# The first modulation set of a transformer block loaded in two halves, with three weight units between them

## The reference

```python
c_act = jax.nn.silu(c)
mod = c_act @ w_ada[l] + b_ada[l]
sh1, sc1, g1, sh2, sc2, g2, sh3, sc3, g3 = jnp.split(mod, N_MOD, axis=-1)
hn = _modulate(_rms(h, norm_ffn1[l]), sh1, sc1)
h = h + 0.5 * g1[:, None, :] * _swiglu(hn, ffn1_w1[l], ffn1_w3[l], ffn1_w2[l])
```

## Time and profile before

| | us |
|---|---|
| median of 3 runs | 2513.48 |
| lowest, highest | 2511.37, 2516.77 |
| the profiled execution's own time | 2513.98 |
| its span | 2512.2 |
| TensorE busy | 2482.2 |
| VectorE busy | 1857.6 |
| ScalarE busy | 1167.3 |
| GpSimd busy | 127.9 |

### The profile page before, as it was taken

How to read it: one execution, slowest core, us unless ns; L and a number is a source line. 1 busy time by engine, 2 the same in 40 slices (tenths; PEclk the granted TensorE clock), 3 DMA queues, 4 the chain that set the end, 5 groups by cost and what they waited for, 6 DMA issues and landing times.

```text
span 2512.2 us, 33153 instructions
## 1 busy us (share of the span) xinstructions
PE 2482.2 (99%) x12155; PEld 2092.3 (83%) x12155; DVE 1857.6 (74%) x2078; ACT 1167.3 (46%) x1423; POOL 127.9 (5%) x198
## 2 busy tenths in 40 slices
PE   7999999999999999999999999999999999999999
PEld 5888888888889999897888888888787888888887
DVE  6876679898978988887865676777689655555556
ACT  4544444444447555655555444344543444444443
POOL 4210000000000000000000000000000000000000
PEclk9999999999999999999999999999999999999999
DMA  9986679999986878875544788786598776676775
GB/s 372 385 277 189 189 256 366 315 361 312 365 284 212 286 257 276 266 224 153 160 141 142 250 263 279 256 297 230 175 350 295 226 209 209 209 209 209 210 211 173
DMA packets 286595, 631.23 MB, mean 251 GB/s; under 512 B 24866, under 2 KB 25476, under 8 KB 285572
## 3 DMA queue, kind: packets, MB, share of 16 engines
q1 hardware_dynamic: 269600, 571.41, 69.2%
q0 software_dynamic: 15120, 53.51, 6.3%
q10 hardware_dynamic: 1748, 4.62, 0.5%
HBM read 616.82 MB, written 12.64 MB: 251 GB/s over the span
## 4 chain that ended last, share of the span: by engine, by line
PE 90%; DVE 5%; DMA 3%; issue 1%; ACT 1%; ACTq 0%; POOL 0%; DVEq 0%
PE psum L2337 26%; PE psum L2339 25%; PE psum L2338 25%; PE psum L2637 3%; PE psum L2639 3%; PE psum L2638 3%; PE psum L2675 2%; DVE w_lo L1472 1%; PE psum L2325 1%; DMA raw<-in_ffn_w 1%; DMA aT_raw<-act_bands 1%; DVE ada_acc L1492 0%; DMA act_bands<-act_blk 0%; DMA gate_mix<-gate_rows 0%; DVE ada_acc L1586 0%
## 5 line engine op out<-in xcount | busy, mean ns | idle before, releaser
L1472 DVE TENSOR_TENSOR w_lo<-raw,w_hi 128x1024 fp32r<-128x1024 f32 (+1 forms) x850 | 1033.6, 1220 | 498.1 <-ACT w_hi L948 496.8
L948 ACT ACTIVATE w_hi<-raw 128x1024 fp32r<-128x1024 f32 (+1 forms) x850 | 898.6, 1060 | 1024.8 <-PE psum L2339 831.2
L2337 PE MATMUL psum<-w_hi,xT_hi 128*128 128x512 f32 x1984 | 783.3, 395 | 3.4 <-issue 2.9
L2339 PE MATMUL psum<-w_hi,xT_lo 128*128 128x512 f32 x1984 | 773.7, 390 | 0.0
L2338 PE MATMUL psum<-w_lo,xT_hi 128*128 128x512 f32 x1984 | 773.5, 390 | 0.0
L2337 PEld LDWEIGHTS psum<-w_hi,xT_hi 128*128 128x128 f32 x1984 | 373.1, 188 | 86.9 <-issue 9.2
L2339 PEld LDWEIGHTS psum<-w_hi,xT_lo 128*128 128x128 f32 x1984 | 373.0, 188 | 78.6
L2338 PEld LDWEIGHTS psum<-w_lo,xT_hi 128*128 128x128 f32 x1984 | 373.1, 188 | 76.3
L2337 PE MATMUL psum<-w_hi,aT_hi 128*128 128x512 f32 x704 | 276.2, 392 | 4.2 <-DVE aT_lo L1745 3.5
L2338 PE MATMUL psum<-w_lo,aT_hi 128*128 128x512 f32 x704 | 275.1, 391 | 0.0
L2339 PE MATMUL psum<-w_hi,aT_lo 128*128 128x512 f32 x704 | 275.0, 391 | 0.0
(11 more groups left out here) (278 smaller groups left out, 2031.9 us busy)
## 6 DMA issues: line engine op xcount, KB each, us to landing
raw<-in_ffn_w SPq DMA_DIRECT2D x528, 512.0 KB, 4.5
ada_raw<-in_w_ada SPq DMA_DIRECT2D x224, 512.0 KB, 5.9
raw<-in_w_in SPq DMA_DIRECT2D x224, 512.0 KB, 3.9
ada_raw<-in_w_ada POOLq DMA_DIRECT2D x32, 512.0 KB, 7.0
ada_more<-in_w_ada POOLq DMA_DIRECT2D x32, 512.0 KB, 7.4
raw<-in_w_br_ssd SPq DMA_DIRECT2D x32, 512.0 KB, 5.5
raw<-in_w_br_att SPq DMA_DIRECT2D x32, 512.0 KB, 4.6
raw<-in_w_out SPq DMA_DIRECT2D x32, 512.0 KB, 5.3
```

The source lines that it names most:

```text
L948: nc.scalar.activation(w_hi[:, n.slot(SPLIT), 0:size], raw[:, n.slot(RAW), 0:size], ACT.Copy).then_inc(hi_ready, 1)
L1472: nc.vector.tensor_tensor(w_lo[:, n.slot(SPLIT), 0:size], raw[:, n.slot(RAW), 0:size], w_hi[:, n.slot(SPLIT), 0:size], ALU.subtract).then_ ...
L2337: nc.tensor.matmul(o, hi[:, kt + k, toks], whi, start=a, stop=False)
L2339: ins = nc.tensor.matmul(o, lo[:, kt + k, toks], whi, start=False, stop=b)
```

## The change

1. Set 0 (tiles 0 to 3) becomes two sets of two tiles (one pair each), of 8 pieces each. A piece still holds 512 KB, now of two tiles of rows by 512 columns, and is loaded with two DMAs of 256 KB and used with two VectorE instructions. There are five sets; the sums go to banks 4, 6, 4, 5, 4. Piece 7 is no longer TensorE's.
2. TensorE transposes two pairs, sums the first half, transposes two more, and does units 0, 1 and 2 (w1 block 0, w3 block 0, w3 block 1, all of pair 0); the other four pairs are transposed in front of units 1, 2 and 3; three warm-ups, the sum of the second half and two warm-ups stand in front of unit 3. The transposes go to banks 6, 7.
3. VectorE's list has the splits of units 0 to 3 behind pieces 7, 9, 11 and 13, ahead of mod_first there. SyncE loads the first units when the pieces before 3, 6, 8 and 11 are used. GpSimd computes the root behind 8 pieces. ScalarE's copies of x are spread between the casts.
4. Another order of units: both first pairs of eight blocks come ahead of the sum for tiles 4 to 7 (now in front of unit 15), then w1 block 4 with four, and w3 block 2, w1 block 3 and w3 block 3 with two more units each. These three are added to their part sums on VectorE. The later sums stand in front of units 30 and 44.

```diff
-ADA_SHARE = (1, 4, 7)
+ADA_SHARE = (1, 4)
...
-    SET_TILES = ((0, 4), (4, 4), (8, 4), (12, 4))
-    SET_START = (0, 16, 32, 48, 64)
+    SET_TILES = ((0, 2), (2, 2), (4, 4), (8, 4), (12, 4))
+    SET_START = (0, 8, 16, 32, 48, 64)
+    SUM_BANK = (4, 6, 4, 5, 4)
...
-    EARLY = (some("w3", 1, (0, 1)) + some("w1", 0, (0,)) + some("w1", 2, (0, 1)) + some("w1", 0, (1,))
-             + some("w3", 2, (0, 1)) + some("w3", 0, (0,)) + some("w1", 3, (0, 1)) + some("w3", 0, (1,))
-             + some("w1", 1, (0, 1))
-             + some("w3", 3, range(4)) + some("w1", 0, (2,)) + some("w1", 4, range(4)) + some("w1", 0, (3,))
-             + some("w3", 0, (2, 3)) + some("w1", 1, (2, 3))
+    EARLY = (some("w1", 0, (0,)) + some("w3", 0, (0,)) + some("w3", 1, (0, 1)) + some("w1", 0, (1,))
+             + some("w1", 2, (0, 1)) + some("w3", 0, (1,)) + some("w3", 2, (0, 1)) + some("w1", 1, (0,))
+             + some("w1", 3, (0, 1)) + some("w3", 3, (0, 1)) + some("w1", 1, (1,))
+             + some("w1", 4, range(4)) + some("w1", 0, (2,)) + some("w3", 2, (2, 3)) + some("w3", 0, (2,))
+             + some("w1", 3, (2, 3)) + some("w1", 0, (3,)) + some("w3", 3, (2, 3)) + some("w3", 0, (3,))
+             + some("w1", 1, (2, 3))
...
-             + some("w3", 2, range(2, UPB)) + some("w1", 3, range(2, UPB)) + some("w2", 2, range(UPB))
-             + some("w3", 3, range(4, UPB)) + some("w1", 4, range(4, UPB)) + some("w2", 3, range(UPB))
+             + some("w3", 2, range(4, UPB)) + some("w1", 3, range(4, UPB)) + some("w3", 3, range(4, UPB))
+             + some("w2", 2, range(UPB)) + some("w1", 4, range(4, UPB)) + some("w2", 3, range(UPB))
...
-    ADDED = [(0, at_unit["w3", 1, 5], 4), (1, at_unit["w1", 2, 5], 4), (0, at_unit["w3", 1, 7], 4),
+    ADDED = [(2, at_unit["w3", 2, 3], 4), (3, at_unit["w1", 3, 3], 4), (4, at_unit["w3", 3, 3], 4),
+             (0, at_unit["w3", 1, 5], 4), (1, at_unit["w1", 2, 5], 4), (0, at_unit["w3", 1, 7], 4),
...
-    SUM_AT = {at_unit["w1", 1, 0]: 1, at_unit["w1", 1, 2]: 2, at_unit["w1", 1, 4]: 3}
+    SUM_AT = {at_unit["w1", 1, 1]: 2, at_unit["w1", 1, 2]: 3, at_unit["w1", 1, 4]: 4}
...
-    SPLIT_AFTER = (14, 16, 17, 18, 20, 21, 22, 23, 25, 26, 27, 28, 31, 32, 33, 34, 35, 36, 37, 38, 39, 41, 42, 43, 44,
-                   46, 47, 48, 49, 50, 51, 52, 53, 54, 55, 57, 58, 59, 60, 62, 63)
-    SCALE_AFTER = (15, 32, 48)
-    ROWS_AFTER = (16, 17, 33, 34, 49, 50)
-    FIRST_UNITS_AFTER = (10, 12, 14, 15)
+    SPLIT_AFTER = (7, 9, 11, 13, 17, 18, 19, 20, 21, 22, 23, 25, 26, 27, 28, 29, 30,
+                   32, 33, 34, 35, 36, 37, 38, 39, 40, 41, 42, 43, 44, 45, 46, 47,
+                   48, 49, 50, 51, 52, 53, 54, 55, 56, 58, 59, 60, 62, 63)
+    SCALE_AFTER = (7, 15, 32, 48)
+    ROWS_AFTER = (8, 17, 33, 34, 49, 50)
+    FIRST_UNITS_AFTER = (3, 6, 8, 11)
...
-        for m in range(ADA_DEEP + 2):
+        for m in range(ADA_DEEP):
             load_first(m)
         pool.wait_ge(sums_ready, 1)
         inverse_root(rstd[:], rbase[:], row_sums[:], D, rstd_ready)
...
-            for j in range(UPB):
+            for j in range(2):
                 stage(0, j)
-            cast_units(2)
+            cast_units(1)
             rows_of_set(0)
-            cast_units(SPLIT)
+            for u in range(1, SPLIT):
+                cast_units(u + 1)
+                for j in (2 * u, 2 * u + 1):
+                    stage(0, j)
+            rows_of_set(1)
...
-                if m == 8:
+                if m == 6:
                     columns()
+                if m in SPLIT_AFTER and m < SET_START[2]:
+                    early_step(SPLIT_AFTER.index(m))
                 if m in SCALE_AFTER:
                     mod_first(SCALE_AFTER.index(m))
                 if m in ROWS_AFTER:
                     lo(0, ROWS_AFTER.index(m))
-                if m in SPLIT_AFTER:
+                if m in SPLIT_AFTER and m >= SET_START[2]:
                     early_step(SPLIT_AFTER.index(m))
...
         share(ADA_SHARE[1])
-        share(ADA_SHARE[2])
         warm_up(1)
         pe.wait_ge(xn_ready, 2)
-        for j in range(UPB):
-            if j >= 2:
-                pe.wait_ge(staged, j - 1)
-            turn_x(0, j, y)
-        for m in (9, 11, 13, 15):
-            pe.wait_ge(ada_used, ada_own(m))
-            warm_up(1)
+        for j in range(2):
+            turn_normed(j)
         sum_first(0)
-        warm_up(2)
+        for j in (2, 3):
+            turn_normed(j)
...
                 if n in SUM_AT:
                     e = SUM_AT[n]
-                    if e < SETS - 1:
-                        pe.wait_ge(part_kept, (4, 6)[e - 1])
+                    if e == 2:
+                        pe.wait_ge(part_kept, 5)
                     else:
-                        pe.wait_ge(part_added, 2)
+                        pe.wait_ge(part_added, 3 if e == 3 else 5)
                     sum_first(e)
+                if n == 1:
+                    turn_normed(4)
+                if n == 2:
+                    turn_normed(5)
+                if n == 3:
+                    turn_normed(6)
+                    turn_normed(7)
+                    pe.wait_ge(staged, UPB)
+                    for m in (11, 13, 15):
+                        pe.wait_ge(ada_used, ada_own(m))
+                        warm_up(1)
+                    sum_first(1)
+                    warm_up(2)
...
+                    if n == at_unit["w3", 2, 2]:
+                        pe.wait_ge(part_kept, 6)
+                    if n == at_unit["w1", 3, 2]:
+                        pe.wait_ge(part_added, 1)
+                    if n == at_unit["w3", 3, 2]:
+                        pe.wait_ge(part_added, 2)
```

More of the change, by code:

```diff
@@ L629, in first_sources_of, with pairs_of_set @@
         return [row[:, :, tile * P:(tile + count) * P] for row in rows]
+    def pairs_of_set(e):
+        tile, count = SET_TILES[e]
+        return range(tile // 2, (tile + count) // 2)
     def landed_first(m):
@@ L679, in turn_bank @@
     def turn_bank(f, j):
-        return (0 if f == 2 else 2) + j % 2
+        return (6, 2, 0)[f] + j % 2
     def twice(cols):
@@ L886, in _ @@
         inverse_root(rstd[:], rbase[:], row_sums[:], D, rstd_ready)
-        for m in range(ADA_DEEP + 2, PIECES):
+        for m in range(ADA_DEEP, PIECES):
             load_first(m)
@@ L1027, in rows_of_set @@
             act.wait_ge(scale_ready, e + 1)
-            for j in (2 * e, 2 * e + 1):
+            for j in pairs_of_set(e):
                 if j >= 2:
@@ L1044, in silu_kept @@
         def silu_kept(o, i):
-            act.wait_ge(part_added, [a[0] for a in ADDED[2:]].index(i) + 3)
+            act.wait_ge(part_added, [a[0] for a in ADDED[PART_SUMS:]].index(i) + PART_SUMS + 1)
             act.wait_ge(prod_ready, o)
@@ L1530, in mod_first @@
             dve.wait_ge(ada_summed, e + 1)
-            nc.vector.tensor_tensor(both(modT), psum[:, 4 + e % 2, 0:2 * count].rearrange("p (c k) -> p c k", c=2),
+            nc.vector.tensor_tensor(both(modT), psum[:, SUM_BANK[e], 0:2 * count].rearrange("p (c k) -> p c k", c=2),
                                     both(badaT), ALU.add).then_inc(mod_ready, 1)
@@ L1768, in add_kept @@
             dve.wait_ge(part_kept, i + 1)
-            if count >= 2 and i < 2:
-                dve.wait_ge(part_added, i + 1)
+            before = [c for c in range(count) if ADDED[c][0] == i]
+            if before:
+                dve.wait_ge(part_added, before[-1] + 1)
             nc.vector.tensor_tensor(kept(i), psum[:, bank:bank + HALF, :], kept(i), ALU.add).then_inc(part_added, 1)
@@ L1788, in early_step @@
                     add_kept(count)
-                    if count >= 2 and KEPT[i][0] == "w3":
+                    if count >= PART_SUMS and KEPT[i][0] == "w3":
                         prod_kept(KEPT[i][1], i, count + 1)
@@ L1895, in ffn @@
             if f == 0:
-                scale_out(1, ADA_MIX)
+                scale_out(1, MORE_SETS + ADA_MIX)
             act_lo(At(o + 1), 0, aT2_hi, aT2_lo)
@@ L2308, in mixer @@
             mods_out(1, 3)
-            scale_out(2, ADA_FFN2)
+            scale_out(2, MORE_SETS + ADA_FFN2)
             merged_lo(At(QB - 1), mT2_hi, mT2_lo, 0)
@@ L2377, in share @@
             pe.wait_ge(first_in[slot], landed_first(m) * 16)
+            cols = 2 * SET_TILES[e][1]
             for j in range(8):
-                ins = nc.tensor.matmul(psum[:, 4 + e % 2, j:j + 1], ada_row(slot)[:, j * P:(j + 1) * P], cact[:, i:i + 1],
+                k, at = i * (8 // cols) + j // cols, j % cols
+                ins = nc.tensor.matmul(psum[:, SUM_BANK[e], at:at + 1], ada_row(slot)[:, j * P:(j + 1) * P], cact[:, k:k + 1],
                                        start=first and j == 0, stop=False, skip_group_check=True)
@@ L2386, in warm_up @@
             for _ in range(count):
-                nc.tensor.matmul(psum[:, 5, :], ident[:], h[:, 0, 0:NB], start=True, stop=True)
```

(21 more changed lines are left out.)

39 lines of the change are left out of this document (20 added, 19 removed).

## The result

The changed kernel takes 2527.47 us (median of 5 runs, 2524.77 to 2529.53) against 2513.48; the ratio is 1.0048, 95% interval 1.0037 to 1.0059, some 12 us slower. The forecast was no measurable change. The profiled execution took 2525.14 us, its span is 2523.4, 11.2 more than before.

What follows compares the result with a forecast made beforehand. TensorE was taken as the bound, neck and neck with VectorE and DMA to about 150 us. +0.3 + 0.5 - 2.7 + 2.1 + 0.6 = +0.8 on 2513.98 gave 2514.8; median 0.5 lower: 2514.3 us, range 2509 to 2520.

Steps and rivals of the forecast that it cites:

- First unit: Start, behind the first half set's sum: unit 0 at 31.2 us, 10.7 earlier than before.
- Unit 3: Behind the second half's sum: begins at 51.0 us against 50.74 before, 0.3 late; 2 us later if its load is late.
- Unit 9's stall gone: Units 3 to 43: unit 9's 1.62 us late start vanishes, part of the -2.7 (bounds -2.7 and 0).
- Unit 33's stall gone: Units 3 to 43: unit 33's 1.09 us wait for VectorE's part sum vanishes, part of the -2.7.
- The evacuation with nothing between, 1.05: Bank 4, between w1 and w3 block 3 and ahead of the next sum: TensorE waits twice, 2 x 1.05 = +2.1.
- Splits run one or two units further ahead: VectorE at each sum in the new order: splits further ahead, the reason for taking both old stalls as gone, -2.7.
- Three more part sums, 0: VectorE's added part sums, 1.22 us each: covered by one other unit between, 0; without cover up to 1.1 each, 3.3.
- +0.6: Between the sums of tiles 4 to 7 and 8 to 11: DMA needs 43.4 us against TensorE's 42.8, +0.6.
- Rival (c): First loads: 256 KB DMAs move slower, 301 GB/s at the lowest, +3 us stay, 2517; chance 0.07.
- Rival (a): Units 13 to 29: slower by the bank 4 ladder, VectorE late, each part sum a stall, +8.0, 2521.5; chance 0.12.
- signs named for a wrong forecast: Unit 3 before 48 or after 54; part sums ending every wait 110-150 us; clock below 0.9; new wait behind 175 us.
- signs for a right one: First unit near 31, unit 3 at 50-52, VectorE idle 21-27, two 1 us holes, last sum 10-12 us after 160.55.

Runs made afterwards that it cites:

- e3: Changed kernel with unit 3 loaded as soon as unit 2 is and the splits of units 33 to 46 behind pieces 50 to 63; 2520.64 us, ratio 1.0021.
- e5: e3 with each evacuation of a part sum ahead of the cast of its step in ScalarE's program; 2518.23 us, ratio 1.0005 to the kernel before.
- e2: Changed kernel with the splits of units 33 to 46 behind pieces 50 to 63 instead of 48 to 62; 2524.53 us, ratio 1.0031.
- e6: Kernel before with each of the first set's 16 pieces loaded as two 256 KB DMAs of two tiles each (runs of 1 KB); 2518.20 us, ratio 1.0009.
- e1: Changed kernel with unit 3 loaded as soon as unit 2 is, instead of behind piece 10; 2527.84 us, ratio 1.0036.
- e7: Kernel before with each of the first set's 16 pieces loaded as two 256 KB DMAs, one per column range (runs of 2 KB); 2515.56 us, ratio 0.9998.

## Why the prediction was wrong

**First unit: right in time, in part by luck.** 31.2 foretold, 30.42 measured. The split that was to be the last step ended at 27.0, but the modulation add then waited 0.50 us more for TensorE's sum. That sum took 3.50 us (from 23.95) and not the 1.95 foretold. VectorE, foretold idle from 21.5 to 27.1, ended piece 7 only at 23.8 and stood 1.94 and 0.50 us.

**Unit 3: right in kind, 2 us off.** The text had 51.0, and 2 us later if unit 3's load landed at twice the median. It was issued at 34.18 and ready at 42.7, 8.5 us, and that bound was what came true: the cast at 42.74 held both the copies of the last pairs (TensorE waited for them until 44.82) and VectorE's split (4.17 us idle), with pieces 14 and 15 behind it. VectorE ended piece 15 at 47.9; the bound had said 48. The landing times of the kernel before in this stretch were there to be read, 8.3 us for the loads issued from 20 to 30 us and 12.9 for those from 30 to 40:

```profile
raw<-in_ffn_w SPq DMA_DIRECT2D x2, 512.0 KB, 8.3
...
raw<-in_ffn_w SPq DMA_DIRECT2D x3, 512.0 KB, 12.9
```

Unit 0 took 5.2 us, 2.5 more than the price of a unit, of which I had added 0.5. Its matmuls start 0.43 us apart instead of 0.23, as they do at the lower level (in e3, where the granted clock was 0.50 at unit 0). In the changed kernel's own profile the granted clock reads 1.00 there, so a spell of low clock is my inference from the spacing.

**Stalls between unit 3 and unit 44: the step that failed.** "I take both as gone: -2.7", "2 x 1.05 = +2.1" and, for the part sums, "0, covered by that unit" came to -0.6 together; measured are 9.0 us of holes against 2.7, +6.3. By item:
- *Unit 9's stall gone*: it is back as unit 11's (1.48), the same evacuation behind a cast that waits for DMA. I had read the mechanism rightly in the earlier trace rows and then assumed that DMA would be ahead.
- *Unit 33's stall gone*: it is back at the same place in the work, now unit 37 (0.93): TensorE starts at 159.31, behind the part sum on VectorE that ran from 158.00.
- *The evacuation with nothing between, 1.05*: 2.21 at unit 13, 4.70 in e3. I priced the evacuation and left out what stands ahead of it on ScalarE, though the same row showed it. e5 moved it and the hole was 1.16. The second one, ahead of the sum, was 1.11, as said.
- *"Splits run one or two units further ahead"*: counted as a gain, it was a loss. Unit 33's split now stood behind piece 48, ahead of the xT_lo, but ScalarE casts unit 33 only behind the rows of that set. VectorE stood 4.42 us, and TensorE paid 0.93 at unit 37 and 2.11 at the last sum. e2 took the first and 1.15 of the second away, for 4 us by the ratios.
- *Three more part sums, 0*: unit 24 waits 0.34, unit 27 nothing: nearly right.

**DMA, "+0.6".** I counted transfers at 387 GB/s. Rival (c) had the mechanism, a lower rate of the new loads, and a price of 3 us; e6 shows 346 GB/s and 2 us, but by the length of the runs, while I argued with the size of the DMAs. The new start also leaves the engines idle at 50 to 60 us (share 0.85). I put that down to VectorE, which had waited for unit 3: pieces and units are asked for only as it uses them, and in e3, where unit 3 is in time, the share there is 1.03.

**Rival (a)** was the nearest in time (2521.5) and has the right place, bank 4, but not the right engine: it was ScalarE's queue, and not VectorE's part sums. The range ended 5 us below the lowest run. Of the signs named for a wrong forecast one came true: a new wait behind 175 us, 2.11 us at the last sum. Of the signs for a right one, unit 3 at 50 to 52, holes of about 1 us at unit 13 and a last sum 10 to 12 us later failed (53.01, 2.21, 20.2 later).

What the runs give together: 12.1 us at 1.0048, of which the earlier load and the later splits give back 6.8 (e3), and the evacuations first 4.0 (e5). What is left, 1.3, is not to be told from nothing, though the runs of 1 KB alone cost 2.3 in e6. These parts aren't independent: with the earlier load unit 13's hole is 4.70 and 5.73 us (e3, e1), where the holes at units 11 and 13 together are 3.69 and 4.39 without it (changed kernel, e2), until e5.

## What to carry to other kernels

Where a start is made earlier by splitting a load, walk each in-order engine's program and ask of each urgent instruction what stands ahead of it and for what that waits: here a late transfer held two engines, and an evacuation of 1.0 us became a hole of up to 5.7 us (e1). Getting one engine further ahead is no gain if its next step waits for a partner that does something else first. Before a load is split, look at how long its contiguous runs become.

## What the runs showed of the hardware

- Loads of 512 KB or 256 KB with 128 partitions moved 380 to 387 GB/s with runs of 2 KB and 346 to 347 with runs of 1 KB, at the same busy share of the DMA engines (1.03 to 1.04; e7 against e6). Halving the size of the DMAs cost nothing.
- GpSimd's issue of a DMA over 128 partitions took 0.74 us for 256 KB and 0.76 for 512 KB, both with two runs for each partition, and 0.55 for 256 KB with one run for each (e7). It followed the number of runs and not the bytes.
- A load of 512 KB landed 4.5 us after its issue over the whole kernel before (median), but after 8.3 and 12.9 us where the DMA engines were full, from 20 to 40 us.
